# A hybrid attention and pooling encoder layer: another order for its first two tiles

## The reference

```python
def encoder_layer(x, norm1_g, w_in, q_norm_g, k_norm_g, w_pool, pool_scale, w_out,
                  norm2_g, w_up, w_down, cos, sin):
    h = rmsnorm(x, norm1_g)                     # over 1024
    proj = h @ w_in                             # 1024 -> 512 q, 128 k, 128 v, 512 u
    q = apply_axial_rope(rmsnorm(q, q_norm_g), cos, sin)   # 8 heads of 64
    k = apply_axial_rope(rmsnorm(k, k_norm_g), cos, sin)   # 2 heads of 64
    a = block_swept_gqa(q, k, v)                # softmax attention, bidirectional
    p = multiscale_pool(u, w_pool, pool_scale)  # windows 2, 4, 8, 16
    x = x + concatenate([a, p]) @ w_out
    h2 = rmsnorm(x, norm2_g)
    return x + square(relu(h2 @ w_up)) @ w_down # 1024 -> 4096 -> 1024
```

## Time and profile before

| | us |
|---|---|
| median of 3 runs | 1545.71 |
| lowest, highest | 1545.16, 1547.87 |
| the profiled execution | 1550.65 |
| its span, first to last instruction | 1548.9 |
| TensorE, VectorE, ScalarE, GpSimd busy | 97%, 67%, 47%, 25% of the span |
| mean granted clock of TensorE | 0.993 of full speed |

### The profile page before, as it was taken

How to read it: one execution, slowest core, us unless ns; L and a number is a source line. 1 busy time by engine, 2 the same in 40 slices (tenths; PEclk the granted TensorE clock), 3 DMA queues, 4 the chain that set the end, 5 groups by cost and what they waited for, 6 DMA issues and landing times.

```text
span 1548.9 us, 23445 instructions
## 1 busy us (share of the span) xinstructions
PE 1501.4 (97%) x8000; PEld 1333.6 (86%) x8000; DVE 1033.5 (67%) x1290; ACT 730.0 (47%) x1231; POOL 391.6 (25%) x337
## 2 busy tenths in 40 slices
PE   6999989999989998999999999999899999999998
PEld 5999877888868887999999999999688888888887
DVE  6533479999976567544544544447688878888875
ACT  5222269999882344545545545546233223223220
POOL 3432577888870001000000000000222311311300
PEclk9999999999999999999999999999999999999999
DMA  6110011000023745643243243247743443443434
GB/s 232 47 46 17 18 69 45 15 10 14 11 79 123 257 181 214 285 151 134 108 151 134 106 153 134 103 156 268 266 150 95 150 150 102 146 153 105 149 97 175
DMA packets 68789, 193.55 MB, mean 125 GB/s; under 512 B 5504, under 2 KB 7680, under 8 KB 68736
## 3 DMA queue, kind: packets, MB, share of 16 engines
q1 hardware_dynamic: 66832, 181.85, 33.4%
q10 hardware_dynamic: 1904, 11.01, 1.7%
HBM read 120.49 MB, written 67.63 MB: 121 GB/s over the span
## 4 chain that ended last, share of the span: by engine, by line
PE 82%; POOL 5%; DVE 4%; issue 3%; ACT 3%; DMA 2%; SPq 0%; ACTq 0%; POOLq 0%; DVEq 0%
PE ps L736 22%; PE ps L738 21%; PE ps L737 21%; PE ps L933 5%; PE ps L834 3%; PE ps L941 3%; POOL prob L2014 2%; DMA hin<-hd 2%; PE ps L849 1%; PE ps L850 1%; PE ps L816 1%; PE ps L818 1%; PE ps L951 1%; POOL sw_prompt L1957 1%; PE ps L745 1%
## 5 line engine op out<-in xcount | busy, mean ns | idle before, releaser
L736 PE MATMUL ps<-h,wuhi 128*128 128x384 f32 x896 | 300.2, 335 | 5.0 <-issue 3.8
L738 PE MATMUL ps<-h,wulo 128*128 128x384 f32 x896 | 299.9, 335 | 0.0
L737 PE MATMUL ps<-h,wuhi 128*128 128x384 f32 x896 | 299.9, 335 | 0.0
L736 PE MATMUL ps<-wdhi,hidhi 128*128 128x512 f32 x672 | 262.6, 391 | 5.9 <-DVE yacc L1854 5.9
L737 PE MATMUL ps<-wdlo,hidhi 128*128 128x512 f32 x672 | 262.2, 390 | 0.0
L738 PE MATMUL ps<-wdhi,hidlo 128*128 128x512 f32 x672 | 262.1, 390 | 0.0
L1854 DVE TENSOR_TENSOR yacc<-yacc,ps 128x1024 f32<-128x1024 f32 x168 | 204.2, 1217 | 82.5 <-PE ps L738 82.4
L1036 ACT ACTIVATE hidhi<-hin 128x1024 fp32r<-128x1024 f32 (+1 forms) x72 | 86.9, 1207 | 312.0 <-PE ps L738 299.1
L1769 DVE TENSOR_TENSOR u<-u,ps 128x384 f32<-128x384 f32 x96 | 53.1, 553 | 186.3 <-PE ps L738 186.2
L736 PEld LDWEIGHTS ps<-h,wuhi 128*128 128x128 f32 x896 | 168.7, 188 | 5.8 <-issue 5.8
L737 PEld LDWEIGHTS ps<-h,wuhi 128*128 128x128 f32 x896 | 168.7, 188 | 0.0
(11 more groups left out here) (171 smaller groups left out, 2892.7 us busy)
## 6 DMA issues: line engine op xcount, KB each, us to landing
hd<-hout SPq DMA_DIRECT2D x64, 384.0 KB, 3.3
hin<-hd SPq DMA_DIRECT2D x48, 512.0 KB, 3.7
hd<-hout SPq DMA_DIRECT2D x32, 576.0 KB, 2.8
hin<-hd SPq DMA_DIRECT2D x24, 768.0 KB, 4.4
wuraw<-in_w_up SPq DMA_DIRECT2D x17, 1024.0 KB, 6.0
wdraw<-in_w_down SPq DMA_DIRECT2D x8, 2048.0 KB, 9.4
h<-h2d ACTq DMA_DIRECT2D x7, 1536.0 KB, 12.5
xin<-in_x SPq DMA_DIRECT2D x12, 512.0 KB, 3.4
```

The lines of the kernel that those rows point to most:

```text
L736: pe.matmul(out, w_hi, m_hi, start=start, stop=False, skip_group_check=resumed)
L737: pe.matmul(out, w_hi, m_lo, start=False, stop=False, skip_group_check=resumed)
L738: return pe.matmul(out, w_lo, m_hi, start=False, stop=stop, skip_group_check=resumed)
```

## The change

The loads are put in another order: `ident` and row 0 of w_in ahead of `g1b`, three more rows ahead of x of tile 1, and x of tiles 2 and 3 later. TensorE's first block is written out (`first_block`). Tile 0 is multiplied row by row as the rows of w_in come (`first_qkv`), with the products of the high part of hT of the first three rows ahead of those of the low part, and with the transposes of tile 1 inside the fifth row. Tile 1 goes into banks 4 and 5 (`second_qkv`), which are those of the pooling projection, its products of the low part last. The transposes of tile 2 follow, and those of tile 3 come ahead of the third group of the pooling projection. That projection waits for the copies out of banks 4 and 5, and row by row for the splits of its columns. ScalarE and VectorE have a `first_pair` each, for tiles 0 and 1, and GpSimd clears `up` behind the first `norm_x` and puts `norm_x(3)` behind the power of tile 0. Loops over blocks are written out. The diff without the parts of `project_block` that only became functions of their own (`copy_qkv`, `square_qk`, `save_u_columns`, `split_v`, `sum_squares`, `norm_qk`, `rotate`):

```diff
+            def load_wi(k):
+                sp.dma_start(wraw[:, k, 0:QKVW], w_in[k * P:(k + 1) * P, 0:QKVW]).then_inc(w_in_in[k], 16)
+
             sp.dma_start(xin[:, 0], x[0:P]).then_inc(x_in[0], 16)
+            sp.dma_start(ident[:], ident_d).then_inc(ident_in, 16)
+            load_wi(0)
             sp.dma_start(g1b[:], g1.partition_broadcast(P)).then_inc(g1_in, 16)
-            sp.dma_start(ident[:], ident_d).then_inc(ident_in, 16)
-            sp.dma_start(wraw[:, 0, 0:QKVW], w_in[0:P, 0:QKVW]).then_inc(w_in_in[0], 16)
+            for k in range(1, 4):
+                load_wi(k)
             sp.dma_start(xin[:, 1], x[P:2 * P]).then_inc(x_in[1], 16)
-            for k in range(1, KT):
-                sp.dma_start(wraw[:, k, 0:QKVW], w_in[k * P:(k + 1) * P, 0:QKVW]).then_inc(w_in_in[k], 16)
-                if k == 4:
-                    load_x(2, 0)
+            for k in range(4, KT):
+                load_wi(k)
+            load_x(2, 0)
             for k in (0, KT // 2):
                 sp.dma_start(wraw[:, k:k + KT // 2, QKVW:],
                              w_in[k * P:(k + KT // 2) * P, QKVW:].rearrange("(k p) n -> p k n", p=P)
                              ).then_inc(w_u_in[k // (KT // 2)], 16)
-            load_x(3, 1)
             sp.dma_start(gqkb[:], gqk.partition_broadcast(P)).then_inc(gqk_in, 16)
             sp.dma_start(rope[:, 0], rope_d[0]).then_inc(rope_in[0], 16)
             sp.dma_start(rope[:, 1], rope_d[1]).then_inc(rope_in[1], 16)
+            load_x(3, 1)
...
+            def first_qkv():
+
+                outs = ((ps[:, 2, :], 0, 512), (ps[:, 3, 0:QKVW - 512], 512, QKVW))
+
+                def high(k):
+                    pe.wait_ge(wi_hi, k + 1)
+                    for out, c0, c1 in outs:
+                        pe.matmul(out, hThi[0][:, k, 0:P], wihi[:, k, c0:c1], start=k == 0, stop=False)
+
+                def cross(k):
+                    for out, c0, c1 in outs:
+                        pe.matmul(out, hTlo[0][:, k, 0:P], wihi[:, k, c0:c1], start=False, stop=False)
+
+                def low(k):
+                    pe.wait_ge(wi_lo, k + 1)
+                    for out, c0, c1 in outs:
+                        mm = pe.matmul(out, hThi[0][:, k, 0:P], wilo[:, k, c0:c1], start=False, stop=k == KT - 1)
+                    return mm
+
+                pe.wait_ge(hT_hi, 1)
+                for k in range(3):
+                    high(k)
+                    low(k)
+                pe.wait_ge(hT_lo, 1)
+                for k in range(3):
+                    cross(k)
+                for k in range(3, KT):
+                    high(k)
+                    cross(k)
+                    if k == 4:
+                        transpose_x(1)
+                    mm = low(k)
+                mm.then_inc(qkv_done, 1)
+
+            def second_qkv():
+
+                outs = ((ps[:, 4, :], 0, 512), (ps[:, 5, 0:QKVW - 512], 512, QKVW))
+                pe.wait_ge(hT_hi, 2)
+                for k in range(KT):
+                    for out, c0, c1 in outs:
+                        pe.matmul(out, hThi[0][:, k, P:2 * P], wihi[:, k, c0:c1], start=k == 0, stop=False)
+                        pe.matmul(out, hThi[0][:, k, P:2 * P], wilo[:, k, c0:c1], start=False, stop=False)
+                pe.wait_ge(hT_lo, 2)
+                for out, c0, c1 in outs:
+                    for k in range(KT):
+                        mm = pe.matmul(out, hTlo[0][:, k, P:2 * P], wihi[:, k, c0:c1], start=False, stop=k == KT - 1)
+                mm.then_inc(qkv_done, 1)
+
+            def first_block():
+                transpose_x(0)
+                first_qkv()
+                second_qkv()
+                transpose_x(2)
+
+                def between(g):
+                    if g == 2:
+                        pe.wait_ge(v_lo, FIRST + 2)
+                        transpose_x(3)
+                    if g == 3:
+                        transpose_qk(0, 0)
+                pe.wait_ge(qk_copied, FIRST + 2)
+                project_u(0, 0, between)
+                transpose_qk(1, 1)
+                project_qkv(2, 2)
+                transpose_x(4)
+                project_qkv(3, 3)
+                transpose_x(5)
+                project_u(1, 1, lambda g: transpose_qk(2, 2) if g == 2 else None)
+                transpose_qk(3, 3)
+
             def project_u(p, buf, between):
                 pe.wait_ge(u_saved, FIRST + p)
-                pe.wait_ge(wi_u_lo, KT)
                 for g in range(GROUPS):
                     between(g)
                     c0 = QKVW + g * P
                     for k in range(KT):
+                        if p == 0 and g == 0:
+                            pe.wait_ge(wi_u_lo, k + 1)
...
-            transpose_x(0)
-            transpose_x(1)
-            with pe.Fori(0, NB - 1) as n:
+            first_block()
+            for n in range(1, NB - 1):
                 project_block(n, False)
...
             square_x(0, 0)
-            split_wi(0)
+            for k in range(3):
+                split_wi(k)
+            split_hT(0, 0)
+            split_wi(3)
             square_x(1, 1)
-            split_hT(0, 0)
-            for k in range(1, 3):
+            for k in range(4, KT):
                 split_wi(k)
             split_hT(1, 1)
-            for k in range(3, 6):
-                split_wi(k)
             square_x(2, 0)
-            for k in range(6, KT):
-                split_wi(k)
-            for k in range(KT):
+            for k in range(KT // 2):
                 split_wi_u(k)
...
+            def first_pair():
+                copy_qkv(0, 2)
+                square_qk(0)
+                for k in range(KT // 2, KT):
+                    split_wi_u(k)
+                square_x(3, 1)
+                copy_qkv(1, 4)
+                split_hT(2, 2)
+                square_qk(1)
+                split_hT(3, 3)
+                square_x(4, 0)
+                save_qkT(0)
+                save_u_columns(0, 1)
+                save_qkT(1)
...
-                for i in range(4):
+                for i in range(2 if isinstance(n, int) and n == 0 else 0, 4):
...
             scale_x(0, 0)
-            split_wi(0)
+            for k in range(3):
+                split_wi(k)
+            split_hT(0, 0)
+            split_wi(3)
             scale_x(1, 1)
-            split_hT(0, 0)
-            for k in range(1, 3):
+            for k in range(4, KT):
                 split_wi(k)
             split_hT(1, 1)
-            for k in range(3, KT):
-                split_wi(k)
             scale_x(2, 0)
-            for k in range(KT):
-                split_wi_u(k)
-            dve.wait_ge(gq_scaled, 1)
...
+            def first_pair():
+                split_v(0, 3)
+                sum_squares(0)
+                for k in range(KT // 2):
+                    split_wi_u(k)
+                dve.wait_ge(gq_scaled, 1)
+                norm_qk(0)
+                for k in range(KT // 2, KT):
+                    split_wi_u(k)
+                split_v(1, 5)
+                split_hT(2, 2)
+                scale_x(3, 1)
+                sum_squares(1)
+                rotate(0, 0)
+                norm_qk(1)
+                split_hT(3, 3)
+                rotate(1, 1)
+                scale_x(4, 0)
...
             norm_x(0)
+            pool.memset(up[:], 0.0).then_inc(pads, 1)
             norm_x(1)
             norm_x(2)
             pool.wait_ge(gqk_in, 16)
             pool.tensor_scalar(gqkb[:, 0:NQ], gqkb[:, 0:NQ], SCALE, 1.0, ALU.mult, ALU.mult
                                ).then_inc(gq_scaled, 1)
-            pool.memset(up[:], 0.0).then_inc(pads, 1)
...
                     t = n * 4 + i
-                    if not (last and i >= 1):
+                    opens = isinstance(n, int) and t == 0
+                    if not (last and i >= 1) and not opens:
                         norm_x(t + 3)
                     pool.wait_ge(qk_summed, FIRST + t + 1)
                     pool.wait_ge(qn_done, FIRST + t)
                     rsqrt_mean(rsqk[:], msqk[:], ssqk[:], epsqk[:], msqk_done, rsqk_done, FIRST + t)
+                    if opens:
+                        norm_x(3)
...
-            with pool.Fori(0, NB - 1) as n:
+            for n in range(NB - 1):
```

More of the change, by code:

```diff
@@ L756, in project_qkv @@
                     for k in range(KT):
-                        if i == 0 and c0 == 0:
-                            pe.wait_ge(wi_lo, k + 1)
                         mm = three(out, hThi[buf][:, k, tok:tok + P], hTlo[buf][:, k, tok:tok + P],
@@ L1111, in exps, with copy_qkv, square_qk @@
                 ins.then_inc(exp_done, 1)
+            def copy_qkv(t, bank):
+                act.wait_ge(qkv_done, t + 1)
+                act.wait_ge(qn_done, FIRST + t)
+                copy(qk[:].rearrange("p h d -> p (h d)"), psw[:, bank * 512:bank * 512 + QKW]).then_inc(qk_copied, 1)
+                copy(V[:, bass.ds(t, 1), :, 0:HEAD].rearrange("p a v d -> p (a v) d"),
```

(55 more changed lines are left out.)

## The result

The changed kernel is slower by 0.2%: the ratio of its time to that of the kernel before is 1.0023 (95% interval 1.0015 to 1.0031), medians 1551.13 and 1546.47 us over 21 runs each. The ratio is 3.6 us on 1546.47, with 2.3 to 4.8 us as its interval; the two medians lie 4.7 us apart. The profiled execution's span is 1551.9 us, against 1548.9.

A forecast was written before the change was run, and what follows sets the result against it. TensorE, busy 97% of the span, was taken as the bound, so only its idle or half-clock stretches could give time back. Ramp -3.4, stall +4.6 and clock +2.1 summed to +3.3 us: 1549.0 us, range 1544.6 to 1551.9.

The forecast's parts named there:

- the ramp: From the start to the pooling projection: reordered loads and first tiles give 3.4 us (2.2 to 4.9).
- the stall: Ahead of transpose_qk(1): TensorE waits for the rotated tile 1, 4.6 us (4.4 to 5.2).
- the clock: TensorE behind its wait for the rotated tile 1: half clock loses 2.1 us, ends 0 and 2.9.
- the slow pace: Half-rate products at the start of TensorE's work: 2.3 us lost, between 1.35 and 3.2.
- the landing of g1b: Gain vector at the start, last of three transfers: lands between 6.3 and 8.6 us, taken as 8.2.
- Cover: TensorE's work from transpose_x(3) to transpose_qk(1): two projection groups and transposes, 7.2 us.
- Chain: From transpose_x(3) through norm_x(4) and tile 1's power to the rotated tile 1: 11.7 to 12.4 us.
- the split would stand inside the chain: split_hT(3) on VectorE, 1.2 us, runs beside the 2.5 us of the sine part before transpose_qk(1).
- Things taken at nothing: First block: qk copy wait (0.1 us at most), pooling-column waits (0 to 0.5), loop control, memset, x of tile 2: zero.
- (A): First pair: ramp gain, stall and half clock together give +3.3 us, own range +1.2 to +5.2; 50%.
- (C): First pair: late g1b, slow pace to 19 or more, longer low clock: -2.2 + 4.8 + 2.9 = +5.5 us; 20%.
- (D): Ahead of transpose_qk(1): no stall, the ramp's gain stands, -3.4 us (-2 to -4.9), 1542.3 us; 10%.

The follow-up runs named there:

- The third experiment: Changed kernel with g1b loaded second again, ahead of ident and row 0 of w_in: ratio 1.0006 to the kernel before.
- The run with two gaps: Changed kernel with the transposes of tile 3 ahead of the second group of the pooling projection instead of the third: ratio 0.9995 to the kernel before.
- the first two edits: Changed kernel with norm_x(4) behind tile 1's power on GpSimd: 0.9984; separately, with square_x(4, 0) ahead of split_hT(3, 3) on ScalarE: 0.9982.
- the run with GpSimd's order: Changed kernel with norm_x of tile 4 behind, not ahead of, the power of tile 1's q and k on GpSimd: ratio 0.9984 to the kernel before.

## Why the prediction was right, point by point

**The time.** +3.3 us was forecast and 3.6 measured (2.3 to 4.8); the measured median, 1551.13, lies in the range, 2.1 us above the 1549.0 of the forecast. The direction and what makes it are right. That the number came out so near is in part luck: the ramp gave 2.0 us less than forecast, the stall cost 0.6 less and the clock 0.2 more, so the terms as measured in the profile add up to 4.9, not 3.3.

**The ramp: mis-sized.** Forecast 3.4 us with bounds 2.2 to 4.9; the projection began at 35.25 for 36.7, so the gain was 1.4 (34.05 to 34.91 in four other kernels with the same ramp: 1.8 to 2.6). The forecast had named this sign itself: if the projection begins after 35, the term of the ramp is wrong. Of the 2.0 us missing, 1.6 are the first product, at 14.07 instead of 12.5, and some 0.5 the slow pace, which lasted 5.5 us behind it where the forecast's 2.3 us of loss stand for 4.6. The step behind the 1.6 is the landing of g1b: "it lands between 6.3 and 8.6", because only three transfers were to be ahead of or beside it. The DMA issues of the changed kernel (KB, us to landing) say otherwise; it was issued at 2.13 and landed at 9.6:

```profile
g1b<-in_g SPq DMA_DIRECT2D x1, 512.0 KB, 7.5
```

The time in which the last of a set had landed before was taken as a bound for another transfer in that place. It isn't one: g1b took 5.1 us from issue to landing when it was second (5.3 in the run that put it back), 7.5 when it was fourth. From its landing on, the steps of the forecast held (xs 1.28 us, transposes 1.94, copy 1.02, first product 1.1 behind the transposes), and the low halves of w_in were hidden, as forecast: TensorE never waited for one. The third experiment shows that with g1b in its old place the first product is at 11.6.

**The stall: right.** Cover 7.2 us: measured from 41.10 to the end of the projection near 48.4, 7.3. Chain 11.8: measured 41.10 to 52.41, 11.3. Wait forecast 4.6, measured 4.0. Of the half microsecond 0.4 lie behind the scaling: from there to the transposes it was 5.4 us before (44.18 to 49.58) and is 5.0 now (47.37 to 52.41). It isn't the shorter sine part, 1.69 us instead of 2.40: the cosine beside its end took 1.40 instead of 0.82 and ended last. The forecast's guess that the split would stand inside the chain and add nothing to it held. That it doesn't depend on the ramp was shown by the run with g1b second (4.0 again), that it comes from the moved transposes by the run of them alone (5.0), and what the chain is by two runs that cut it at different links (1.0) and one that left it and added cover (0).

**The clock: right.** Forecast a drop worth 2.1 us. The nine products at 0.43 us instead of 0.23 lose 1.8, and the five transposes 0.5. The run with two gaps puts it at 2.1, the run of the moved transposes alone at 2.4. The rule of the Trainium skill (TensorE: Matmul & The Clock Gate, "Why this matters for your kernels"), that an idle stretch between bursts puts the engine back to half rate, is borne out by the gaps of 4.0 and 5.0 us, each with half clock behind it; gaps of 1.8, 1.1 and 1.0 us in the same place had none.

**The rest.** -1.4 + 4.0 + 2.3 = +4.9, and the profile shows 5.1 at tile 7. From 60 to 180 us nothing but that shift is there, as forecast; the first product of tile 2 is at 53.39, later than the 50.5 to 52.5 given, by what the ramp lacked. The ratio over many runs says 3.6 and the two spans are 3.0 apart. Half-clock stretches and waits of later stages fall differently in each execution (the waits near 1100 us are 2.7 us shorter in the changed kernel's), and the ramp is often better than in the profiled execution of the changed kernel. How much of the difference between 5.1 and 3.6 is the one and how much the other stays open. Things taken at nothing were at nothing: the copy of q and k ahead of the projection (0.2 us), the pooling columns row by row, the memset, x of tile 2. The loops are not settled, as said.

**The rivals.** The case is (A) in size, with the small ramp of (C): g1b at 8.6 or later (9.6) and the slow pace to 19 or more (19.6). (D), no stall, is what the first two edits make of it: 0.9984 and 0.9982, 2.5 to 2.8 us faster than before, where it was put at -3.4; in both 1.0 us of waiting is left.

## What to carry to other kernels

When a step is moved to a later place in one engine's queue, look for who waits for it in the queues of the others, through orders that stay as they are: here a norm that nobody needed soon stood ahead of a power that was needed at once, and had done no harm only because the step that fed it came early. Compare, from the moved step on, the length of that chain with the work left to cover it; the difference is the stall, whatever is won ahead of it. And a load needed first should stay first even if a bigger batch behind it seems to be what the engine works on.

## What the runs showed of the hardware

- A gap of TensorE of 4 to 5 us cost half as much again: 2.1 to 2.4 us at half clock behind it, in all three kernels profiled with such a gap at this place. 3.0 us of idle time in two parts of 1.8 and 1.1 us cost only itself.
- The half pace at the start ended 2.7 us after the first product in the kernel before, 3.1 after it (at about 17.3 us) in the run with GpSimd's order, and 5.5 after it (at 19.6) in the profiled execution of the changed kernel, which has the same ramp. So the start of the projection differs by 1 us (34.2, 35.25) between executions with the same ramp. The Trainium skill (TensorE: Matmul & The Clock Gate, "PE-mode transpose") says that transposes don't count toward full speed; nothing here contradicts it or shows it.
- The same power on 128 x 10 numbers took 1.96 us on GpSimd with VectorE idle, 1.97 where VectorE was in the split of hT, which reads PSUM, as it started, and 2.3 to 2.9 where VectorE was in an operation on two SBUF operands. The sine part took 1.7 us beside the split and 2.4 with the cosine started at the same time; behind the split, the cosine took 1.4 instead of 0.8 while the sine part ran. That operations on two SBUF operands and those of GpSimd hold each other up fits all these rows, and no run isolated it.
